# Two-layer hybrid transformer with a routed expert layer, one core: TensorE's and the sync engine's programs for the expert waves written out instead of looped, and down products taken two chunks at a time

## The reference, cut to what matters

```python
D_MODEL, N_EXPERTS, TOP_K, D_FF_EXPERT = 1024, 8, 2, 3584

def swiglu(h, wg, wu, wd):
    return (jax.nn.silu(h @ wg) * (h @ wu)) @ wd

def moe_swiglu(h, w_router, wg, wu, wd):
    t = h.reshape(-1, shp[-1])                    # 256 tokens x 1024
    top_v, top_i = lax.top_k((t @ w_router).astype(F32), TOP_K)
    gates = jax.nn.softmax(top_v, axis=-1)
    for e in range(N_EXPERTS):
        w_e = jnp.sum(jnp.where(top_i == e, gates, 0.0), axis=-1)
        out = out + w_e[:, None] * swiglu(t, wg[e], wu[e], wd[e])
```

## Time and profile before

| | us |
|---|---|
| median of 3 runs | 2281.72 (2277.76 to 2283.62) |
| time of the profiled execution | 2278.74 |
| its span in the profile | 2276.8 |
| TensorE busy | 2000.3 (88%) |
| weight transfers of the expert layer | 64 x 3 of 1792 KB, median 19.0 to 21.2 us from issue to landing |
| first gate/up product of wave 0, last down product of wave 7 | 1315.7, 2254.5 |

### The profile page before, as it was taken

The page is one execution under the profiler, slowest core; times in us unless marked ns, Lnnn a source line. Parts: engine busy times, 40 slices in busy tenths (PEclk is TensorE's granted clock), DMA queues, the critical chain, the costliest instruction groups (busy, mean ns, idle before and its releaser), DMA issues.

```text
span 2276.8 us, 24303 instructions
## 1 busy us (share of the span) xinstructions
PE 2000.3 (88%) x9801; PEld 1197.1 (53%) x9802; DVE 624.3 (27%) x1274; ACT 526.5 (23%) x853; POOL 401.7 (18%) x241
## 2 busy tenths in 40 slices
PE   4999778968899998979899698998988899888786
PEld 2787335956677767868665443343433344333332
DVE  3933356644100014450054320110211100111012
ACT  3332224543221221232133110110211110211021
POOL 0431530532233433435221000000000000000000
PEclk8999879979899998989999799999999999999998
DMA  8443000112345451223353679877999978799995
GB/s 313 148 155 119 1 0 1 38 74 74 112 161 208 149 187 72 93 74 111 94 41 25 258 279 415 343 290 262 401 407 418 402 296 301 284 417 407 416 409 223
DMA packets 147117, 482.68 MB, mean 212 GB/s; under 512 B 23268, under 2 KB 48213, under 8 KB 132645
## 3 DMA queue, kind: packets, MB, share of 16 engines
q1 hardware_dynamic: 145984, 477.89, 56.4%
q10 hardware_dynamic: 997, 2.75, 0.3%
HBM read 479.56 MB, written 1.05 MB: 211 GB/s over the span
## 4 chain that ended last, share of the span: by engine, by line
PE 60%; DMA 8%; DVE 4%; issue 2%; ACT 2%; SPq 1%; POOL 0%; DVEq 0%; ACTq 0%; POOLq 0%
PE PS L2239 20%; DMA BIG<-in_od_exp_wu 8%; PE PS L1753 7%; PE PS L1754 7%; PE PS L1755 7%; PE PS L2285 7%; PE PS L2167 2%; PE PS L1948 1%; PE PS L2215 1%; PE PS L2230 1%; PE PS L2087 1%; DVE HB L1190 1%; SPq L547 1%; PE PS L2169 1%; PE PS L1732 1%
## 5 line engine op out<-in xcount | busy, mean ns | idle before, releaser
L2239 PE MATMUL PS<-BIG,QB 128*64 128x448 f32 x2560 | 516.1, 562 | 72.4 <-issue 41.9
L2239 PEld LDWEIGHTS PS<-BIG,QB 128*64 128x64 f32 x2560 | 185.3, 142 | 383.3 <-issue 375.7
L2285 PE MATMUL PS<-BIG,QB 128*64 128x512 f32 x1120 | 245.5, 593 | 1.3 <-DMA BIG<-in_od_exp_wd 0.7
L587 POOL TENSOR_TENSOR BIG_parts<-BIG,QB_parts 128x2048 fp32r<-128x2048 f32 x33 | 152.7, 4627 | 282.8 <-ACT QB_parts L746 282.8
L587 POOL TENSOR_TENSOR BIG_parts<-BIG,BIG_parts 128x2048 fp32r<-128x2048 f32 (+1 forms) x28 | 126.1, 4503 | 248.3 <-ACT BIG_parts L746 248.3
L2285 PEld LDWEIGHTS PS<-BIG,QB 128*64 128x64 f32 x1120 | 89.5, 137 | 151.3 <-issue 148.6
L1754 PE MATMUL PS<-HB_parts,QB_parts 128*128 128x512 f32 x352 | 137.3, 390 | 0.0
L1669 DVE TENSOR_TENSOR HB<-HB,PS 128x512 f32<-128x512 f32 x36 | 24.8, 688 | 380.4 <-PE PS L2215 380.4
L1754 PE MATMUL PS<-BIG_parts,BIG_parts 128*128 128x512 f32 (+1 forms) x336 | 127.4, 379 | 0.0
L1753 PE MATMUL PS<-ZS_parts,BIG_parts 128*128 128x512 f32 (+1 forms) x240 | 92.5, 385 | 10.0 <-DVEq L1200 8.1
L1755 PE MATMUL PS<-BIG_parts 128*128 128x512 f32 (+1 forms) x256 | 96.3, 376 | 0.0
(11 more groups left out here) (340 smaller groups left out, 3052.0 us busy)
## 6 DMA issues: line engine op xcount, KB each, us to landing
BIG<-in_od_exp_wg SPq DMA_DIRECT2D x64, 1792.0 KB, 19.0
BIG<-in_od_exp_wu SPq DMA_DIRECT2D x64, 1792.0 KB, 21.2
BIG<-in_od_exp_wd SPq DMA_DIRECT2D x64, 1792.0 KB, 21.1
BIG<-in_ada_w SPq DMA_DIRECT2D x24, 2048.0 KB, 8.1
BIG<-in_od_w_qkv SPq DMA_DIRECT2D x6, 2048.0 KB, 7.9
BIG<-in_ev_ffn_wg SPq DMA_DIRECT2D x11, 1024.0 KB, 8.8
BIG<-in_ev_ffn_wu SPq DMA_DIRECT2D x11, 1024.0 KB, 11.3
BIG<-in_ev_ffn_wd SPq DMA_DIRECT2D x5, 2048.0 KB, 8.8
```

The costliest lines, as they stand in the source:

```text
L587: pool.tensor_tensor(r12(w), w, r12(high), ALU.subtract).then_inc(split_l, 1)
L2239: last = mm(PS[at:at + 64, bank, 0:GROUP], XG[:, 4 * part + k, r0:r0 + 64], wgu[u][:, k, GROUP * c:GROUP * c + GROUP], start=(part + k == ...
L2285: last = mm(PS[64 * n:64 * n + 64, bank, :], HET[:, 7 * q + k, c0:c0 + 64], slot_e[:, a, :], start=(q + k == 0), stop=(q == NPAIR - 1 and ...
```

## The change

TensorE: the waves 0 to 6 are written out one after another with constants in place of `w`; their seven `more` values are read into seven registers ahead of wave 0. Wave 7 and any above it stay a loop. Down products: TensorE now waits for both down chunks of a pair, then does 14 products for the upper rows (if `more`) and 14 for the lower ones, and counts `dn_mm` once a pair (4 a wave, not 8). SP: the loads of waves 1 to 7 are written out; the load into slot i waits for the pair i // 2.

```diff
-                        sp.wait_ge(dn_mm, NDN * w + i - NDN + 1)
+                        sp.wait_ge(dn_mm, NPAIR * (w - 1) + i // 2 + 1)
...
-            with sp.Fori(1, E) as w:
+            for w in range(1, E):
                 wave_loads(w, w, False)
...
-                act.wait_ge(dn_mm, NDN * w + NDN)
+                act.wait_ge(dn_mm, NPAIR * w + NPAIR)
...
+            more_than_half = [pe.value_load(RIB[0:1, w:w + 1], min_val=0, max_val=1) for w in range(E - 1)]
             pe.wait_ge(e_sel, 1)
             gather(0, 0)
             gather(0, 1)
-            with pe.Fori(0, waves) as w:
-                more = pe.value_load(RIB[0:1, bass.ds(w, 1)], min_val=0, max_val=1)
+            def wave(w, more):
...
-                for i in range(NDN):
-                    slot_e = arrive(w, 2 * NUP + i).rearrange("p (a n) -> p a n", n=512)
-                    q = i // 2
+                for q in range(NPAIR):
+                    halves_of = [arrive(w, 2 * NUP + 2 * q + i).rearrange("p (a n) -> p a n", n=512) for i in range(2)]
                     pe.wait_ge(e_htev, NPAIR * w + q + 1)
-                    def down(bank, c0):
-
-                        for a in range(7):
-                            k, n = (7 * (i % 2) + a) // 2, (7 * (i % 2) + a) % 2
-                            last = mm(PS[64 * n:64 * n + 64, bank, :], HET[:, 7 * q + k, c0:c0 + 64], slot_e[:, a, :],
-                                      start=(q + k == 0), stop=(q == NPAIR - 1 and k == 6))
+                    def down(bank, r0):
+
+                        for i in range(2):
+                            for a in range(7):
+                                k, n = (7 * i + a) // 2, (7 * i + a) % 2
+                                last = mm(PS[64 * n:64 * n + 64, bank, :], HET[:, 7 * q + k, r0:r0 + 64],
+                                          halves_of[i][:, a, :], start=(q + k == 0), stop=(q == NPAIR - 1 and k == 6))
                         return last
                     with pe.If(more > 0):
                         down(7, 64)
                     down(6, 0).then_inc(dn_mm, 1)
+
+            for w in range(E - 1):
+                wave(w, more_than_half[w])
+            with pe.Fori(E - 1, waves) as w:
+                wave(w, pe.value_load(RIB[0:1, bass.ds(w, 1)], min_val=0, max_val=1))
             scatter(waves)
```

## The result

The changed kernel takes 2262.61 us (median of 4 runs, 2260.57 to 2266.04), the kernel before 2281.56 us (4 runs): a ratio of 0.9918, with a 95% interval of 0.9904 to 0.9933, 19 us faster. Run once more beside three others, on one chip, it gave 0.9937 (0.9924 to 0.9949), 2266.23 us. The profiled execution took 2266.04 us, its span is 2264.2, 12.6 less than before.

The account below looks back on a forecast made before the run. Transfers stalling behind long waves 1 and 4 were taken to cost time. The terms -9.3 - 10.5 + 2.6 + 2.3 gave -14.9 us, so 2266.8 us against the median before of 2281.7; range 2257 to 2277.

Parts of the forecast that it names:

- What bounds it: Behind long waves 1 and 4 transfers stall while TensorE restarts; time saved there stays saved, as transfers bound what follows.
- First restart: Between waves 1 and 2: without the branch back, slots come free and transfers resume earlier, a gain of 9.3 us.
- second: Between waves 4 and 5: the same earlier restart of the transfers, a gain of 10.5 us.
- Seven reads: Register loads ahead of the first gather delay wave 0 and the transfers, a loss of 2.6 us.
- Slots in pairs: Each pair's first chunk goes out one half later, hidden by SP's deep queue: 0; uncovered, 15 us.
- Down products wait for both chunks: Hidden in wave 3; at the end of wave 7 the last pair finishes later, a loss of 2.3 us.
- The other boundaries: Behind waves 0, 2, 3, 5 and 6 the missing branch back gains 0, hidden by gapless transfers.
- SP, 0: Writing out SP's loop changes nothing: issues wait on products or a full queue, not on SP's arithmetic.
- the 6.55 and 4.55 us: TensorE's jump back and first taken branch behind wave 1, slow as if the code there had to be fetched.
- The window of two pages: Skill's rule: prefetch is sequential, and a taken branch outside the current window waits for a DMA of that page.
- Rival B: Written-out code stalls 3 to 5 us at taken branches whose target isn't there; slower, 2303 or 2357 us; chance 0.05.

Follow-up runs that it names:

- experiment 1: Against the kernel before: only TensorE's waves written out; down products, slot waits and SP's loop as before. 2261.54 us, ratio 0.9921.
- experiment 3: The changed kernel with its waves as three loops (0 to 1, 2 to 4, 5 to 7), no branch back behind waves 1 and 4. 2263.82 us, ratio 0.9926.
- experiment 4: The changed kernel with loops over waves 1 to 2 and 4 to 5, so branches back only behind the long waves. 2260.27 us, ratio 0.9915.
- experiment 5: The kernel before with 97 empty instructions at TensorE's start, putting its wave loop in 7 blocks of 256 instructions. 2252.16 us, ratio 0.9873.
- 7: The changed kernel with the seven register reads moved behind the first gather. 2259.75 us, ratio 0.9911 to the kernel before.
- 8: The changed kernel with the last wave's down chunks taken singly as each lands. 2260.1 us, ratio 0.9909 to the kernel before.
- experiment 9: The changed kernel measured again, unaltered, beside three others on one chip. 2266.23 us, ratio 0.9937 to the kernel before.
- 10: The changed kernel with the seven register reads done twice ahead of the first gather. 2266.07 us, ratio 0.9947 to the kernel before.
- experiment 11: The kernel before with down products, waits and counts in pairs, and 97 empty instructions putting TensorE's loop in 7 blocks. 2256.99 us, ratio 0.99.
- experiment 12: The kernel before with 97 empty instructions (TensorE's loop in 7 blocks), single down chunks, and SP's loop written out. 2252.06 us, ratio 0.989.
- 2: The kernel before with down products, slot waits and counts in pairs, both loops kept. 2282.22 us, ratio 1.0019.
- 6: The kernel before with 224 empty instructions (128 at the start, 96 ahead of the expert layer), TensorE's loop over 8 blocks. 2291.58 us, ratio 1.0056.

## Why the prediction was right

The forecast was 2266.8 us with a range of 2257 to 2277; measured 2262.6 and 2266.2. Step by step:

- **What bounds it** (the transfers stand still behind the long waves, and a microsecond saved there stays saved): shown. All kernels without the slow branch there (changed, 1, 3 to 5 and 7 to 12) are faster by 12 to 30 us, those with it (2 and 6) are not.
- **First restart, -9.3, second, -10.5:** measured -9.1 and -10.2.
- **Seven reads, +2.6:** measured +2.4 up to wave 0's first product, and +4.7 for seven more. That the delay costs as much of the time was argued; the medians could not confirm it.
- **Slots in pairs, 0:** nearly right. The flow at the restart is 337 GB/s, 407 behind it, with no gap of the size feared (3.1 us at each boundary). With pairs the two stretches behind the long waves are 0.6 to 1.2 us longer each (changed kernel against experiment 1, experiment 11 against 5).
- **Down products wait for both chunks, +2.3:** undersized, measured +4.6. The waiting came out as forecast in kind, but I let the last pair start at the landing and run warm in 6.2 us; it starts 0.66 us behind it and takes 7.89, TensorE having idled 2.6 us. In experiment 1, with single chunks, the end takes 3.9 us as before.
- **Not in the sum, -3.0 and -1.6:** the long waves start faster. Before, TensorE idles over 5 us ahead of wave 1 and its first 64 records take 15.1 us, those of wave 4 13.7, where both take 12.25 in the changed kernel:

```profile
1409.37 15.13 PE PS L2239 x64
...
1780.87 13.71 PE PS L2239 x64
```

  Now the wait for the last down chunk comes earlier, and TensorE's idle time falls ahead of wave 0's last pair, which takes 7.93 us where a warm one takes 6.23:

```profile
1407.29 7.93 PE L2286 MATMUL PS<-BIG,QB 128*64 128x512 f32 x28 [2.35 <-issue]
```

  The granted clock over 1409 to 1417 is 0.85, in the kernel before 0.61. A part of the clock's cost moved from a wave where time counts to one where it is hidden. It comes with the pairs: wave 1 takes 161.5 and 161.7 us in experiments 1 and 5, 158.7 in 11. The second gain is less sure, since wave 4 takes 160.6 in experiment 9's profile of the changed kernel.
- **The other boundaries, 0; SP, 0:** right (experiment 12 for SP).

The +2.3 that the last pair costs more and the -4.6 that the long waves give back partly cancel, and the profile's difference without its first line is -16.9 (in the second profile -14.1) beside a forecast of -14.9. That the sum came so close is in part luck.

The step that was right for a wrong reason is the cause of the stall. The prediction took the 6.55 and 4.55 us for what a branch back costs and wrote "as if the code there had to be fetched". What costs is the fetch and not the branch: the second loop of experiment 3 and both of experiment 4 branch back in 0.2 us, and experiments 5 and 6 switch the stall off and on by where the loop lies. The window of two pages that the prediction took over from the Trainium skill, "Runtime: NRT & Kernel Launch", section "Instruction fetch mechanics", is not borne out: in experiment 4 a branch back over 6.5 blocks took 0.22 us. Writing the waves out was one way to be rid of it; it needed none of the rest. Rival B (stalls at taken branches in the written-out code) didn't come: 64 branches, 0.37 us at most.

## What to carry to other kernels

Where the chain shows "issue" behind a loop's end, look at the sequencer's branch and at the packets of the instruction queue: if they go on through every pass, the loop is fetched anew each time, and some empty instructions in a place where the engine waits, or a slightly shorter body (not tried here), may do what writing it out does. Look at what the empty instructions cost themselves: 0.15 us each here. Price such a stall only where nothing else covers it: here seven boundaries had it and two counted. When an experiment puts the suspected cost back and nothing happens, look for what differs between its instances before defending the theory.

## What was not expected of the hardware

- A loop of 1663 or 1670 instructions on TensorE was run again without any fetch where it lay in 7 blocks of 256 by the count above, and fetched anew where it lay in 8. In experiment 5 the last packet of instructions comes during wave 0.
- Without instruction fetches the two long stretches behind waves 1 and 4 are shorter still. From the end of wave 1 to the landing of wave 4's second chunk, and from the end of wave 4 to the last landing: changed kernel 200.4 and 299.3 us, experiment 1 199.8 and 298.5, experiment 5 196.8 and 295.0. Part of it may be the earlier free slots of single down chunks, which experiment 1 has too; some 3 us of each go with the fetches (experiments 1 and 5 both have single chunks). With pairs the first stretch goes with their number too: 200.4, 199.3, 198.9 and 198.0 us in the changed kernel and experiments 4, 3 and 11, with 12, 7, 6 and 0 packets of instructions in it. By what path was not tried.
- Code that no kernel of the study touches scatters: the router's first product starts at 1283.2 to 1293.4 us in the profiled executions of the kernels without empty instructions, 1284.0 before and 1288.3 after. Differences under some 5 us of two single profiles mean nothing without such a landmark.
